# A decoder layer in one program: the order of stick-breaking steps, memory attention and dilated attention on TensorE

## The chip, the core and the metric

The kernel runs on one core of a Trainium2 chip. The metric is the device time of one execution in microseconds (us), median of several. A core has five engines with queues of their own: TensorE (PE in the profile, its weight loads PEld), VectorE (DVE), ScalarE (ACT), GpSimd (POOL) and SyncE (SP, which issues most transfers here). The engines wait for each other through semaphores, and each works through its own list strictly in the order in which it is written. TensorE multiplies a stationary tile of weights with a moving tile of columns into PSUM, which has four pairs of banks here (`ps[:, 0]` to `ps[:, 3]`, 1024 fp32 columns each).

## The reference

One layer over x (1024 positions, 1024 features), all in fp32:

```
x = x + 0.5 * swiglu(rmsnorm(x), ffn1)
h = rmsnorm(x);  q_sb,k_sb,v_sb, q_d,k_d,v_d, q_x, gates = split(h @ w_in)
A (stick-breaking, 6 heads of 64):  z = q k^T / 8
   a = where(s < t, exp(log_sigmoid(z) + sum over s' > s of log_sigmoid(-z)), 0);  o = a v
B (dilated attention, 3 groups x 2 heads, QK-norm, relative bias), combined by softmax denominators
C (memory attention, 4 heads, 256 tokens, QK-norm):  softmax(q mk^T) mv
merged = sum over branches of sigmoid(gate) * (o @ w_branch);  x = x + merged @ w_out
x = x + 0.5 * swiglu(rmsnorm(x), ffn2)
```

## The kernel before

Activations lie transposed (features on partitions, positions along the columns). A projection product takes each fp32 operand as a high and a low part in the fp32r type and adds three products (high by high, low by high, high by low); for one 128-row tile `k` of the contraction and 1024 positions that is six matmuls of 512 columns. Weights come one unit (128 x 1024) at a time: SyncE fetches `raw`, ScalarE writes its high part (`split_hi`), VectorE the low part (`split_lo`, line 1011), two units ahead.

The mixer has three stretches that concern us, each written out by hand as one list per engine.

**Stick-breaking** (36 steps `s`, three pairs of heads with 12 steps each). A step treats one block of 128 keys of two heads against up to 512 queries. The position inside its pair (0 to 11) sets the width of a head's part: 128, 256, 384, then five times 512, then 128, 256, 384, 512. A step consists of
- scores (`sb_scores`, TensorE, six matmuls with 64 rows, into `ps[:, s % 2]`); they wait for `sb_kept`, ScalarE's copy of the scores two steps earlier,
- ScalarE's |z|, exp, copy and ln (`sb_explog`), with two masks on GpSimd in the blocks on the diagonal; VectorE's softplus, high and low part (`sb_softplus`, lines 1277, 1284, 1286),
- `sb_within`: four matmuls with a triangle of ones that add to the running sum in `ps[:, 2]`; VectorE's add of that sum to the scores (`sb_add`, line 1293); ScalarE's exp of it, the weights (`sb_weights`, line 845),
- `sb_carry`: four more matmuls that complete the running sum; they wait for the add. VectorE may write the high part of step s+2 only behind them (line 1283),
- `sb_values`: weights by values, in fp32, two heads side by side of 64 columns each; they wait for the weights.

Beside the steps runs a projection of nine units: `beside(s, i, j)` multiplies tiles i to j of half a unit, three matmuls of 512 columns a tile, four tiles a step. Its result lies in one bank, which VectorE copies out at the end of each second step (`beside_copy`, line 1314). In that same bank values are turned (`v_turn`, copied out by `v_out`) and sums of squares of the memory queries are formed (`xq_sum`, copied out by `xq_keep`, followed by `xq_scale`).

**Memory attention** (8 pieces `n`) beside eight projections of 1024 positions: `x_turn` (eight fp32 transposes of the weights), `x_scores(n + 1)`, `x_values(n)`. Weights of piece n+1 are ready when VectorE has divided them (`x_divide`).

**Dilated attention** (32 blocks `n`) beside `fill(n)`, one contraction tile of a gate product: `d_scores` for two blocks at a time, `d_turn`, `d_values` for two blocks.

Of the kernel before, what the change touches and what calls it, by code (L numbers as in the profile page):

```python
# [25 lines left out]
P = 128  # L26
D = 1024
S = 1024
# [179 lines left out]
def is_v(half):  # L208
    return half is not None and half // 2 % 3 == 2
# [16 lines left out]
def layer(nc, x, mem, weights, gains, head_gains, rel_bias, consts, onehot, out):  # L226
    ctx = ExitStack()
    with ctx:
        base = -(-nc.sbuf_base // 64) * 64

        def at(name, off, shape, dt=F32):
            return nc.alloc_sbuf_tensor_at(name, shape, dt, offset=base + off)
# [79 lines left out]
        sp_hi = at("sp_hi", XT + 8 * K, [P, 2, 2, 512], F32R)  # L312
        sp_lo = at("sp_lo", XT + 16 * K, [P, 2, 2, 512], F32R)

        sb_a = [at(f"sb_a{i}", o, [P, 2, 512]) for i, o in enumerate((XT + 24 * K, XT + 28 * K, AR + 48 * K, AR + 28 * K))]

        tri = at("tri", MISC + 512, [P, 2, P], F32R)

# [93 lines left out]
        def after(eng, s, value):  # L412

            if not isinstance(value, int) or value > 0:
                eng.wait_ge(s, value)
# [35 lines left out]
            return ps[:, s % 2, :].rearrange("p (h c) -> p h c", h=2)  # L451

        def sb_weights_of(s):
            return sb_a[3 if s % 3 == 2 and s >= 2 * PAIR_STEPS else s % 3]

        def carry(h):

# [21 lines left out]
        def bank(i):  # L479
            return ps[:, i // 2, (i % 2) * 512:(i % 2) * 512 + 512]  # L480
# [153 lines left out]
        def _(act):  # L634
# [59 lines left out]
            def proj_square(n):  # L694

                kind, w = PROJ[n]
                pr_sq, pr_rs, pr_vT = pr_mem if n < PR_SB else pr_x
                if kind == "norm" and n >= PR_DIL:
                    act.wait_ge(pr_copied, n + 1)
                    after(act, pr_kept, kept_before(n))  # L700
                    nc.scalar.activation(sq_full[:], proj_dest(n), ACT.Square).then_inc(pr_sq_done, 1)
                    nc.scalar.activation(sq_hi[:], proj_dest(n), ACT.Square).then_inc(pr_sq_hi_done, 1)
                elif kind == "norm":
                    act.wait_ge(pr_copied, n + 1)

                    after(act, pr_final, aux_before(n))
                    nc.scalar.activation(pr_sq[:, 0:w], proj_dest(n), ACT.Square).then_inc(pr_sq_done, 1)
                elif kind == "copy":
                    act.wait_ge(pr_copied, n + 1)
                    nc.scalar.activation(sb_qk[:, 0, 2 * (n - PR_SB), :], proj_dest(n), ACT.Copy).then_inc(qk_hi_done, 1)  # L710
# [115 lines left out]
            def sb_explog(s):  # L826

                l, z = sb_l[:, s % 2, :, sb_step(s)[3]:], sb_scores_of(s)[:, :, sb_step(s)[3]:]
                act.wait_ge(sb_z, s + 1)
                after(act, sb_lo, s - 1)  # L830
                nc.scalar.activation(l, z, ACT.Abs).then_inc(sb_abs, 1)  # L831
                act.wait_ge(sb_abs, s + 1)
                nc.scalar.activation(l, l, ACT.Exp, scale=-1.0).then_inc(sb_exp, 1)  # L833
                after(act, sb_av, s - 2)
                nc.scalar.activation(sb_weights_of(s)[:, :, sb_step(s)[3]:], z, ACT.Copy).then_inc(sb_kept, 1)
                act.wait_ge(sb_exp, s + 1)
                if on_edge(s):
                    act.wait_ge(sb_exp_masked, edges_before(s) + 1)
                nc.scalar.activation(l, l, ACT.Ln, bias=1.0).then_inc(sb_ln, 1)
# [65 lines left out]
            for n in range(9):  # L905
                p = PR_DIL + n
                if n == 1:
                    act.wait_ge(xq_final, 4)
                if n:
                    proj_square(p - 1)  # L910
                if n < 8:
                    split_hi(proj_unit(p) + AHEAD)
                if n < 8:
                    for b in range(MB):
                        act.wait_ge(xa_turned, 2 * n + b + 1)
                        after(act, xa_pv, n)
                        nc.scalar.activation(x_pT[:, b, :], ps[:, 1, 512 * b:512 * b + 512], ACT.Copy).then_inc(xa_pT, 1)
                if n + 1 < 8:
                    x_exp(n + 1)
                if n:  # L920
                    proj_keep(p - 1)
                if n:
                    proj_rstd(p - 1)
# [81 lines left out]
        def _(dve):  # L1005
# [255 lines left out]
            def x_divide(n):  # L1261
                dve.wait_ge(xa_exp, 4 * n + 4)
                nc.vector.reciprocal(x_rden[:], x_den[:]).then_inc(xa_rden, 1)
                dve.wait_ge(xa_rden, n + 1)
                nc.vector.tensor_tensor(x_p[:], x_p[:], x_rden[:].unsqueeze(2).to_broadcast([P, 4, MEM]),
                                        ALU.mult).then_inc(xa_prob, 1)
# [117 lines left out]
            for n in range(9):  # L1384
                p = PR_DIL + n
                behind = n > 1 and PROJ[p - 2][0] == "norm"
                if behind and PROJ[p - 1][0] == "turn":
                    proj_final(p - 2)
                if n:
                    proj_copy(p - 1)  # L1390
                if behind and PROJ[p - 1][0] == "norm":
                    proj_final(p - 2)
                if n < 8:
                    split_lo(proj_unit(p) + AHEAD)
                if n == 0:
                    xq_scale(2)
                    xq_scale(3)
                if n + 1 < 8:
                    x_lowest(n + 1)
                    x_divide(n + 1)  # L1400
                if n < 8:
                    pair, quarter = divmod(n, 4)
                    dve.wait_ge(xa_pv, n + 1)
                    nc.vector.tensor_copy(o_x[:, pair, 256 * quarter:256 * quarter + 256], bank(2)[:, 0:256]).then_inc(xa_o, 1)
                if 0 < n < 8 and PROJ[p - 1][0] == "turn":
                    proj_final(p - 1)

# [138 lines left out]
        def _(pe):  # L1546
# [297 lines left out]
            def sb_scores(s):  # L1844

                p, c, j, a = sb_step(s)
                after(pe, sb_kept, s - 1)
                if s % PAIR_STEPS == 0:
                    pe.wait_ge(qk_done, 2 + 4 * p)
                for i, (k, q) in enumerate(((2, 0), (2, 1), (3, 0))):  # L1850
                    for h in range(2):
                        r = h * HD
                        last = mm(ps[:, s % 2, 512 * h + a:512 * h + 512], sb_qk[r:r + HD, p % 2, k, j * P:(j + 1) * P],
                                  sb_qk[r:r + HD, p % 2, q, 512 * c + a:512 * c + 512], i == 0, i == 2)
                last.then_inc(sb_z, 1)
# [75 lines left out]
                mm(xq_bank(q), head_r[:], xq_sq_lo[:, half_of(q)[1]], False, True).then_inc(xq_sums, 1)  # L1931

            proj(PR_SB, hh, hl)
            norm_sum(1)
            proj(PR_SB + 1, hh, hl)
            proj(PR_SB + 2, hh, hl)

            def x_scores(n):
# [12 lines left out]
            sb_scores(0)  # L1951
            sb_scores(1)
            proj_aux(PR_SB + 2)
            beside(0, 0, 4)
            for s in range(SB_STEPS):
                if s + 2 < SB_STEPS:
                    sb_scores(s + 2)
                if is_v(half_done(s - 1)):
                    v_turn(half_done(s - 1))
                if xq_at(s) is not None:  # L1960
                    xq_sum(xq_at(s))
                early = 0 if not s or is_v(half_done(s - 1)) or xq_at(s) is not None else 2
                if early:
                    beside(s, 0, early)
                if s:
                    sb_carry(s - 1)
                    sb_values(s - 1)
                if s:
                    beside(s, early, 4)
                else:  # L1970
                    pe.wait_ge(pr_final, aux_before(PR_DIL))
                sb_within(s)
# [43 lines left out]
            for n in range(8):  # L2016
                if n == 1:
                    pe.wait_ge(sb_o, 6)
                    pe.wait_ge(bs_v, 6)
                proj(PR_DIL + n, hh, hl, k1=DT // 2)  # L2020
                if n == 0:
                    sb_values(SB_STEPS - 1)
                x_turn(n)
                if n < 7:
                    x_scores(n + 1)
                proj(PR_DIL + n, hh, hl, k0=DT // 2, k1=DT - 2)
                if n:
                    proj_aux(PR_DIL + n - 1)
                x_values(n)
                proj(PR_DIL + n, hh, hl, k0=DT - 2)  # L2030

            pe.wait_ge(xa_exp, 32)
# [43 lines left out]
            for n in range(DN):  # L2076
                if n % 2 == 0 and n + 2 < DN:
                    d_scores(n + 2)
                if n % 8:
                    fill(n)  # L2080
                d_turn(n)
                if n == 2:
                    pe.wait_ge(pr_final, aux_before(len(PROJ)))
                if n % 2 == 0 and n:
                    d_values(n - 2)
                if n % 8 == 0 and n:
                    fill(n)
            d_values(DN - 2)

# [143 lines left out]
```

## Time and profile before

| what | us |
|---|---|
| median of 3 runs | 2343.32 (2341.65 to 2344.09) |
| the profiled execution's own time | 2342.55 |
| its span | 2340.8 |
| TensorE busy in the span | 2312.7 |
| stick-breaking loop, from 805.1 to 1027.3 | 222.2 |
| memory attention beside projections, from 1027.3 to 1150.0 | 122.7 |
| dilated attention, from 1150.0 to 1234.4 | 84.4 |

The granted clock of TensorE is 1.00 in all three stretches. A row of the timeline gives the start of a group of like instructions, how long the group takes and what the engine waited for; matmuls overlap, so what a group costs its engine is read from the start of the next row, not from its length.

### The profile page before, as it was taken

Reading aid. Unit: us, or ns where it says so; the run is one execution under the profiler, and the core shown is the slowest. Engines: PE = TensorE matmul, PEld = TensorE weight load, DVE = VectorE, ACT = ScalarE, POOL = GpSimd, SP = SyncE. Lnnn points to the kernel's source line nnn. Section 1 sums busy time; section 2 is a strip of 40 time slices with the busy share of each in tenths; the row PEclk is TensorE's granted clock in tenths of the full one; section 3 lists DMA queues with packets and bytes.
Section 4 is the critical chain, followed back from the end, with each engine's and each line's share of the span. In section 5 each row is a group of like instructions: output and inputs, shape, how many; then the busy total and the mean of one; then the engine's idle time right before and its main releaser. Section 6 shows DMA issues by size and latency. Waiting matters only on the chain.

```text
span 2340.8 us, 25824 instructions
## 1 busy us (share of the span) xinstructions
PE 2312.7 (99%) x10616; PEld 1859.5 (79%) x10616; DVE 1148.9 (49%) x1119; ACT 620.4 (27%) x800; POOL 137.6 (6%) x108
## 2 busy tenths in 40 slices
PE   8999999999999999999999999999999999999998
PEld 7888888888887766667778888888888888888887
DVE  8443444443445677777636343445344434444434
ACT  6211111111112567756443111223111111111111
POOL 3000000000001321212000000011000000000000
PEclk9999999999999999999999999999999999999999
DMA  5211111111112200001122111131111111111112
GB/s 161 76 45 54 45 49 40 54 45 54 45 54 61 108 28 19 19 28 55 37 28 64 54 54 45 55 117 53 47 52 48 45 54 45 48 42 54 45 54 72
DMA packets 47424, 125.78 MB, mean 54 GB/s; under 512 B 4285, under 2 KB 20829, under 8 KB 47104
## 3 DMA queue, kind: packets, MB, share of 16 engines
q1 hardware_dynamic: 45456, 112.61, 15.9%
q10 hardware_dynamic: 912, 10.11, 1.1%
q0 software_dynamic: 992, 2.15, 0.5%
q8 instruction: 48, 0.79, 0.1%
q14 instruction: 16, 0.13, 0.0%
HBM read 116.42 MB, written 9.87 MB: 54 GB/s over the span
## 4 chain that ended last, share of the span: by engine, by line
PE 93%; DVE 5%; ACT 1%; issue 1%; POOL 0%; DMA 0%; SPq 0%; DVEq 0%; ACTq 0%
PE ps L1548 91%; DVE h_lo L1018 1%; DVE w_lo L1011 0%; DVE sb_a L1293 0%; PE ps L2041 0%; DVE xT L1082 0%; DVE xT L1194 0%; DVE h_lo L1474 0%; PE ps L1984 0%; PE ps L2135 0%; DMA raw<-in_weights 0%; ACT sb_a L845 0%; ACT sb_l L833 0%; ACT sb_l L831 0%; PE ps L1757 0%
## 5 line engine op out<-in xcount | busy, mean ns | idle before, releaser
L1548 PE MATMUL ps<-h_hi,w_hi 128*128 128x512 f32 x2240 | 876.7, 396 | 2.7 <-ACT w_hi L641 2.3
L1548 PE MATMUL ps<-h_lo,w_hi 128*128 128x512 f32 x2240 | 862.6, 390 | 0.8 <-DVE h_lo L1474 0.4
L1548 PE MATMUL ps<-h_hi,w_lo 128*128 128x512 f32 x2240 | 699.9, 390 | 0.0
L1548 PEld LDWEIGHTS ps<-h_hi,w_hi 128*128 128x128 f32 x2240 | 420.2, 188 | 128.0 <-issue 40.5
L1548 PEld LDWEIGHTS ps<-h_hi,w_lo 128*128 128x128 f32 x2240 | 420.8, 188 | 88.9
L1548 PEld LDWEIGHTS ps<-h_lo,w_hi 128*128 128x128 f32 x2240 | 420.3, 188 | 85.8 <-DVE h_lo L1474 1.7
L641 ACT ACTIVATE w_hi<-raw 128x1024 fp32r<-128x1024 f32 x196 | 204.2, 1051 | 791.5 <-PE ps L1548 771.0
L1011 DVE TENSOR_TENSOR w_lo<-raw,w_hi 128x1024 fp32r<-128x1024 f32 x196 | 249.7, 1282 | 159.1 <-ACT w_hi L641 150.2
L1082 DVE TENSOR_TENSOR xT<-xT,ps 128x1024 f32<-128x1024 f32 x175 | 213.3, 1219 | 181.2 <-PE ps L1548 181.2
L1548 PE MATMUL ps<-a_hi,w_hi 128*128 128x512 f32 x704 | 276.8, 393 | 5.6 <-DVE w_lo L1011 4.9
L1548 PE MATMUL ps<-a_lo,w_hi 128*128 128x512 f32 x704 | 275.1, 391 | 0.0
L1548 PE MATMUL ps<-a_hi,w_lo 128*128 128x512 f32 x704 | 218.1, 391 | 0.0
L1048 DVE SCALAR_TENSOR_TENSOR glu<-ps,rB 128x1024 f32<-128x1024 f32 x44 | 53.9, 1224 | 265.1 <-PE ps L1548 265.1
L1041 DVE TENSOR_TENSOR silu<-ps,rB 128x1024 f32<-128x1024 f32 x44 | 53.8, 1224 | 252.1 <-PE ps L1548 252.1
L677 ACT ACTIVATE silu<-silu 128x1024 f32<-128x1024 f32 x44 | 46.6, 1060 | 439.6 <-DVE silu L1041 439.6
L1548 PEld LDWEIGHTS ps<-a_hi,w_hi 128*128 128x128 f32 x704 | 133.1, 189 | 35.3 <-DVE w_lo L1011 5.7
L1548 PEld LDWEIGHTS ps<-a_hi,w_lo 128*128 128x128 f32 x704 | 132.7, 189 | 27.8
L1548 PEld LDWEIGHTS ps<-a_lo,w_hi 128*128 128x128 f32 x704 | 133.0, 189 | 27.1
L567 POOL TENSOR_TENSOR acc<-acc,sq 128x1024 f32<-128x1024 f32 x21 | 51.9, 2470 | 1090.5 <-ACT sq L648 1090.5
L1414 DVE TENSOR_TENSOR gate<-ps,rB 128x1024 f32<-128x1024 f32 x24 | 29.4, 1224 | 128.2 <-PE ps L1548 128.2
L941 ACT ACTIVATE gate<-gate 128x1024 f32<-128x1024 f32 x24 | 25.0, 1058 | 172.7 <-DVE gate L1414 172.5
L1066 DVE TENSOR_TENSOR glu<-glu,silu 128x1024 f32<-128x1024 f32 x44 | 53.9, 1224 | 4.4
(224 smaller groups left out, 1589.4 us busy)
## 6 DMA issues: line engine op xcount, KB each, us to landing
raw<-in_weights SPq DMA_DIRECT2D x196, 512.0 KB, 3.5
x_keep<-xT ACTq DMA_DIRECT2D x1, 4096.0 KB, 12.3
x_back<-x_keep ACTq DMA_DIRECT2D x1, 4096.0 KB, 13.4
x_nat<-in_x SPq DMA_DIRECT2D x7, 512.0 KB, 7.4
out<-y_nat SPq DMA_DIRECT2D x7, 512.0 KB, 3.2
toe_keep<-toe_row ACTq DMA_DIRECT2D x2, 704.0 KB, 6.1
m_nat<-in_mem SPq DMA_DIRECT2D x1, 1024.0 KB, 8.4
d_fB<-d_f_keep POOLq DMA_DIRECT2D x2, 512.0 KB, 6.5
```

What stands on the lines that cost most here:

```text
L567: nc.gpsimd.tensor_tensor(acc[:], acc[:], sq[:, k % 2, :], ALU.add).then_inc(acc_done, 1)
L641: nc.scalar.activation(w_hi[:, k % NW].rearrange("p a b -> p (a b)"), raw[:, k % NRAW, :], ACT.Copy).then_inc(hi_done, 1)
L677: nc.scalar.activation(silu[:, t % 2, :], silu[:, t % 2, :], ACT.Silu).then_inc(silu_done, 1)
L941: nc.scalar.activation(gate_tile(m, b), gate_tile(m, b), ACT.Sigmoid).then_inc(gate_done, 1)
L1011: nc.vector.tensor_tensor(w_lo[:, k % NW].rearrange("p a b -> p (a b)"), raw[:, k % NRAW, :], w_hi[:, k % NW].rearrange("p a b -> p (a b)" ...
L1018: nc.vector.scalar_tensor_tensor(out=h_lo[:, k, :], in0=xT[:, k, :], scalar=g32[:, gain, k:k + 1], in1=h_hi[:, k, :].bitcast(F32), op0=ALU ...
L1041: nc.vector.tensor_tensor(silu[:, t % 2, :], ps[:, 0, :], rB[:], ALU.mult).then_inc(gate_scaled, 1)
L1048: nc.vector.scalar_tensor_tensor(out=glu[:, t % 2, :], in0=ps[:, 1, :], scalar=0.5, in1=rB[:], op0=ALU.mult, op1=ALU.mult).then_inc(up_sca ...
L1066: nc.vector.tensor_tensor(glu[:, t % 2, :], glu[:, t % 2, :], silu[:, t % 2, :], ALU.mult).then_inc(glu_done, 1)
L1082: nc.vector.tensor_tensor(xT[:, m, :], xT[:, m, :], ps[:, 2 + m % 2, :], ALU.add).then_inc(down_added, 1)
L1414: nc.vector.tensor_tensor(gate_tile(m, b), ps[:, merge_pair(m, b), :], rB[:], ALU.mult).then_inc(mg_taken, 1)
L1548: return pe.matmul(o, a, b, start=start, stop=stop, skip_group_check=True)
```

## The change

In the stick-breaking loop the scores of two steps and the values of two steps now stand together at the beginning of each even step. The tiles of the projection move accordingly (three between carry and within in even steps, three ahead of the carry and two behind it in odd ones). Six buffers for weights in place of four, and one of its own for the last step. The first tile of projection `PR_SB + 1` goes ahead of the norm's sum. In memory attention the turn stands behind the first tile of a projection (from the second one on), and the values directly behind the next scores; ScalarE's copies of the turned weights and VectorE's copy of the result move ahead. In dilated attention the values of two blocks stand directly behind the scores of two blocks, and each `fill` stands behind a turn. The values of the last two steps are in the middle of the first projection of the next stretch.

```diff
+        sb_a = [at(f"sb_a{i}", o, [P, 2, 512])
+                for i, o in enumerate((XT + 24 * K, XT + 28 * K, AR + 48 * K, AR + 52 * K, AR + 28 * K, AR + 32 * K))]
+        sb_a_end = at("sb_a_end", AR + 14 * K, [P, 2, S])[:, :, 0:512]
         def sb_weights_of(s):
-            return sb_a[3 if s % 3 == 2 and s >= 2 * PAIR_STEPS else s % 3]
+            if s == SB_STEPS - 1:
+                return sb_a_end
+            return sb_a[s % 4 + (2 if s % 4 > 1 and s >= 2 * PAIR_STEPS else 0)]
...
-                after(act, sb_av, s - 2)
+                after(act, sb_av, s - 3)
...
             proj(PR_SB, hh, hl)
+            proj(PR_SB + 1, hh, hl, k1=1)
             norm_sum(1)
-            proj(PR_SB + 1, hh, hl)
+            proj(PR_SB + 1, hh, hl, k0=1)
...
-            beside(0, 0, 4)
+            beside(0, 0, 3)
             for s in range(SB_STEPS):
-                if s + 2 < SB_STEPS:
+                odd = s % 2
+                if not odd and s + 2 < SB_STEPS:
                     sb_scores(s + 2)
+                    sb_scores(s + 3)
+                if not odd and s:
+                    sb_values(s - 2)
+                    sb_values(s - 1)
                 if is_v(half_done(s - 1)):
                     v_turn(half_done(s - 1))
                 if xq_at(s) is not None:
                     xq_sum(xq_at(s))
-                early = 0 if not s or is_v(half_done(s - 1)) or xq_at(s) is not None else 2
-                if early:
-                    beside(s, 0, early)
+                if odd:
+                    beside(s, -1, 2)
                 if s:
                     sb_carry(s - 1)
-                    sb_values(s - 1)
                 if s:
-                    beside(s, early, 4)
+                    beside(s, 2 if odd else 0, 4 if odd else 3)
                 else:
                     pe.wait_ge(pr_final, aux_before(PR_DIL))
                 sb_within(s)
...
-                proj(PR_DIL + n, hh, hl, k1=DT // 2)
+                proj(PR_DIL + n, hh, hl, k1=1)
+                if n:
+                    x_turn(n)
+                proj(PR_DIL + n, hh, hl, k0=1, k1=DT // 2)
                 if n == 0:
+                    sb_values(SB_STEPS - 2)
                     sb_values(SB_STEPS - 1)
-                x_turn(n)
+                if n == 0:
+                    x_turn(n)
                 if n < 7:
                     x_scores(n + 1)
+                if n:
+                    x_values(n)
...
-                x_values(n)
+                if n == 0:
+                    x_values(n)
...
-                if n % 8:
-                    fill(n)
-                d_turn(n)
                 if n == 2:
                     pe.wait_ge(pr_final, aux_before(len(PROJ)))
                 if n % 2 == 0 and n:
                     d_values(n - 2)
-                if n % 8 == 0 and n:
+                d_turn(n)
+                if n:
                     fill(n)
```

TensorE's list before, from the carry of step 14 to the beginning of step 16 (`sb_qk` are scores, `sb_a` by `sb_v` values, `sp` by `tri` carry or within, `h` by `w` tiles of the projection):

```order
L1548 MATMUL ps<-sp_lo,tri 128x384 x2
L1548 MATMUL ps<-sb_a_106,sb_v_100 64x384 x2
L1548 MATMUL ps<-h_hi,w_hi 128x512
...
L1548 MATMUL ps<-h_hi,w_lo 128x512
L1548 MATMUL ps<-sp_hi,tri 128x512 x2
L1548 MATMUL ps<-sp_lo,tri 128x512 x2
L1548 MATMUL ps<-sb_qk 128x512 x6
L1548 MATMUL ps<-h_hi,w_hi 128x512
```

Values and scores each stand alone there, with tiles or a carry around them. The same place now, from the carry of step 14 to that of step 15:

```order
L1556 MATMUL ps<-sp_lo,tri 128x384 x2
L1556 MATMUL ps<-h_hi,w_hi 128x512
...
L1556 MATMUL ps<-h_hi,w_lo 128x512
L1556 MATMUL ps<-sp_hi,tri 128x512 x2
L1556 MATMUL ps<-sp_lo,tri 128x512 x2
L1556 MATMUL ps<-sb_qk 128x512 x12
L1556 MATMUL ps<-sb_a_106,sb_v_100 64x384 x2
L1556 MATMUL ps<-sb_a_107,sb_v_100 64x512 x2
L1556 MATMUL ps<-sp_hi,tri 128x512 x2
```

The scores of two steps (x12) and the values of two steps stand behind each other between a within and a carry; before, each stood alone between other kinds.

TensorE's list in dilated attention before, between two turns of three blocks each (`cst` by `d_p` are turns, `d_qk` scores, `d_pT` by `d_v` values):

```order
L2041 MATMUL ps<-cst,d_p 128x128 x3
L1548 MATMUL ps<-d_qk 128x128 x2
L1548 MATMUL ps<-d_qk 128x256 x2
L1548 MATMUL ps<-h_hi,w_hi 128x512
...
L1548 MATMUL ps<-h_hi,w_lo 128x512 x2
L2041 MATMUL ps<-cst,d_p 128x128 x3
L1548 MATMUL ps<-d_pT,d_v 64x128 x6
```

Each turn has scores or values behind it, and these a fill. The same stretch now:

```order
L1556 MATMUL ps<-d_qk 128x256 x2
L1556 MATMUL ps<-d_pT,d_v 64x128 x6
L2061 MATMUL ps<-cst,d_p 128x128 x3
L1556 MATMUL ps<-h_hi,w_hi 128x512
...
L1556 MATMUL ps<-h_hi,w_lo 128x512 x2
L2061 MATMUL ps<-cst,d_p 128x128 x3
L1556 MATMUL ps<-h_hi,w_hi 128x512
```

Scores, values and a turn follow each other, and the other turn stands alone between two fills.

## Rows read from the trace of the kernel before

**Rows 1.** The page, busy us, share of the span, instructions.

```profile
PE 2312.7 (99%) x10616; PEld 1859.5 (79%) x10616; DVE 1148.9 (49%) x1119; ACT 620.4 (27%) x800; POOL 137.6 (6%) x108
```

**Rows 2.** Windows, the stick-breaking loop: busy us and count by engine, clock.

```profile
805.10:1027.30 222.20, 216.35 (x1057) 145.09 (x1056) 167.91 (x198) 160.81 (x209) 48.30 (x49) 1.00 0.07 22
```

**Rows 3.** Waits of PE, 770 to 1250: us in total, times, longest.

```profile
PE ps L1548 <- ACT sb_a L845: 4.0, 6, 1.1
PE ps L1548 <- POOL acc_lo L570: 1.6, 1, 1.6
PE ps L1548 <- DVE sb_a L1293: 1.2, 2, 1.0
PE ps L1548 <- ACT d_pT L823: 0.6, 1, 0.6
```

**Rows 4.** Timeline of PE: start us, length us, group, count [idle before].

```profile
905.98 0.97 PE L1548 MATMUL ps<-sb_qk 64*128 64x512 f32 x6
906.88 0.50 PE L1548 MATMUL ps<-h_hi,w_hi 128*128 128x512 f32 x1
907.22 0.40 PE L1548 MATMUL ps<-h_lo,w_hi 128*128 128x512 f32 x1
...
908.37 0.61 PE L1548 MATMUL ps<-sp_hi,tri 128*128 128x512 f32 x2
908.82 0.61 PE L1548 MATMUL ps<-sp_lo,tri 128*128 128x512 f32 x2
909.37 1.08 PE L1548 MATMUL ps<-sb_a,sb_v 128*64 128x512 f32 x4
910.38 0.50 PE L1548 MATMUL ps<-h_hi,w_hi 128*128 128x512 f32 x1
```

**Rows 5.** Timeline of PE: two scores together, and each kind alone.

```profile
799.94 0.96 PE L1548 MATMUL ps<-sb_qk 64*128 64x128 f32 x12
...
912.88 0.55 PE L1548 MATMUL ps<-sb_qk 64*128 64x128 f32 x6
...
919.36 0.62 PE L1548 MATMUL ps<-sb_qk 64*128 64x256 f32 x6
```

**Rows 6.** Timeline behind a within of 512 columns.

```profile
874.66 0.79 PE L1548 MATMUL ps<-sb_qk 64*128 64x384 f32 x6
874.77 1.22 DVE L1293 TENSOR_TENSOR sb_a<-sb_a,ps 128x1024 f32<-128x1024 f32 x1 [0.21 <-PE ps L1548]
...
877.13 1.08 PE L1548 MATMUL ps<-sb_a,sb_v 128*64 128x512 f32 x4 [1.10 <-ACT sb_a L845]
```

**Rows 7.** Timeline: from a carry's end (the values' start) through VectorE's list.

```profile
895.80 0.87 PE L1548 MATMUL ps<-sb_a,sb_v 128*64 128x384 f32 x4
...
899.58 1.21 DVE L1293 TENSOR_TENSOR sb_a<-sb_a,ps 128x1024 f32<-128x1024 f32 x1
...
902.48 1.08 PE L1548 MATMUL ps<-sb_a,sb_v 128*64 128x512 f32 x4
...
903.38 1.23 DVE L1286 TENSOR_TENSOR sp_lo<-sb_l,sp_hi 128x1024 fp32r<-128x1024 f32 x1
```

**Rows 8.** Timeline of DVE, steps 30 and 31: sums kept, next add.

```profile
989.60 0.69 DVE L1336 COPY xq_kept_sums<-ps 128x512 f32<-128x512 f32 x1
...
997.75 1.21 DVE L1293 TENSOR_TENSOR sb_a<-sb_a,ps 128x1024 f32<-128x1024 f32 x1
```

**Rows 9.** Lines, 805 to 1027: busy us, mean ns of one, idle before.

```profile
L1286 DVE TENSOR_TENSOR sp_lo<-sb_l,sp_hi 128x1024 fp32r<-128x1024 f32 x18 | 24.7, 1371 | 0.6
```

**Rows 10.** Timeline of DVE, from the last result to the second piece's weights.

```profile
1035.57 0.69 DVE L1300 COPY o_sb<-ps 128x512 f32<-128x512 f32 x1 [2.35 <-PE ps L1548]
...
1045.64 1.23 DVE L1265 TENSOR_TENSOR x_p<-x_p,small 128x1024 f32<-128x1024 f32 x1
```

**Rows 11.** Timeline of PE in dilated attention, a turn ahead of scores.

```profile
1195.22 0.49 PE L2041 MATMUL ps<-cst,d_p 128*128 128x128 f32 x3
1195.64 0.93 PE L1548 MATMUL ps<-d_qk 64*128 64x128 f32 x8
```

More of the change, by code:

```diff
@@ L313, in layer @@
         sp_lo = at("sp_lo", XT + 16 * K, [P, 2, 2, 512], F32R)
-        sb_a = [at(f"sb_a{i}", o, [P, 2, 512]) for i, o in enumerate((XT + 24 * K, XT + 28 * K, AR + 48 * K, AR + 28 * K))]
+        sb_a = [at(f"sb_a{i}", o, [P, 2, 512])
+                for i, o in enumerate((XT + 24 * K, XT + 28 * K, AR + 48 * K, AR + 52 * K, AR + 28 * K, AR + 32 * K))]
+        sb_a_end = at("sb_a_end", AR + 14 * K, [P, 2, S])[:, :, 0:512]
         tri = at("tri", MISC + 512, [P, 2, P], F32R)
@@ L908, in _ @@
                     act.wait_ge(xq_final, 4)
-                if n:
-                    proj_square(p - 1)
-                if n < 8:
+                if n == 0:
                     split_hi(proj_unit(p) + AHEAD)
@@ L917, in _ @@
                         nc.scalar.activation(x_pT[:, b, :], ps[:, 1, 512 * b:512 * b + 512], ACT.Copy).then_inc(xa_pT, 1)
+                if n:
+                    proj_square(p - 1)
+                if 0 < n < 8:
+                    split_hi(proj_unit(p) + AHEAD)
                 if n + 1 < 8:
@@ L1399, in _ @@
                     x_lowest(n + 1)
-                    x_divide(n + 1)
                 if n < 8:
@@ L1404, in _ @@
                     nc.vector.tensor_copy(o_x[:, pair, 256 * quarter:256 * quarter + 256], bank(2)[:, 0:256]).then_inc(xa_o, 1)
+                if n + 1 < 8:
+                    x_divide(n + 1)
                 if 0 < n < 8 and PROJ[p - 1][0] == "turn":
@@ L2028, in _ @@
                     proj_aux(PR_DIL + n - 1)
-                x_values(n)
+                if n == 0:
+                    x_values(n)
                 proj(PR_DIL + n, hh, hl, k0=DT - 2)
@@ L2085, in _ @@
                     d_values(n - 2)
-                if n % 8 == 0 and n:
+                d_turn(n)
+                if n:
                     fill(n)
```

## The prediction, made before the changed kernel ran

> **What bounds the kernel now.** I read the page first: TensorE is busy for 2312.7 of 2340.8 us [rows 1], so anything that doesn't shorten TensorE's list, or a wait in it, is worth nothing. Then the windows: in the stick-breaking loop TensorE is busy for 216.4 of 222.2 us, but VectorE has 167.9 and ScalarE 160.8 [rows 2], so they have a quarter of slack and no more. The list of waits says that TensorE waits little there, 4.0 us for weights and 1.2 us for adds, besides one wait of 1.6 us at the norm's sum and one of 0.6 us at the end of dilated attention [rows 3]. The busy share hides a cost, though, which only the starts in the timeline show. Inside one kind of full-width matmul the starts are 0.23 us apart (two in 0.45, from 908.37 to 908.82). The two before values take 0.55, so 0.10 more; six scores, which run as three pairs of heads, take 0.90 in place of 0.69; and the first projection matmul behind them takes 0.34 in place of 0.23 [rows 4]. So scores that stand alone cost 0.10 + 0.20 + 0.11 = 0.4 us beyond their columns. For values I take as bare time 0.213 us for each 128 columns, the step between 0.87 and 1.08 us, the lengths at 384 and 512 columns [rows 7]; 512 columns are 0.85, the row takes 1.01 [rows 4], and with the ends the overhead is 0.10 + 0.16 + 0.11, some 0.36 us.
>
> **Stick-breaking, what is saved.** Before, two steps hold two scores and two values apart: 2 x 0.40 + 2 x 0.36 = 1.52 us of overhead. Now there is one island. Two scores in a row exist in one place: twelve matmuls of 128 and 256 columns have a length of 0.96, the two alone 0.55 and 0.62, of which 0.07 is tail, so 1.10 together [rows 5]. That join saves 0.14 us beyond the ends, which I extend to wide ones at up to 0.2. Scores directly ahead of values don't exist in the trace: between 0 and 0.2 us; I take 0.15, since going from either kind to the full width costs about 0.2 [rows 4]. An island then costs 0.10 + 0.10 + 0.05 + 0.15 + 0.05 + 0.11, about 0.57, and two steps save 0.95. There are 16 such islands (steps 2 to 32), 15.2 us, and the ends of the loop (step 0, step 34, values of step 34 in the next stretch) give 0.35 each: **16.3 us saved**.
>
> The page TensorEngine Tiling (Array Packing) of the Trainium skill, section Key Properties, says that a change of the tiling mode drains TensorE while a change of tile within a mode does not. By that rule the joins of like kinds are free and the step from scores to values (other rows and columns) is not, as I take it; without a drain there the loop would gain 16 x 0.15 = 2.4 us more. No row here decides it.
>
> **Stick-breaking, what is lost.** The values of an odd step s-1 now stand a short way behind its own within. What must happen meanwhile is add, weights exp, and that takes 877.13 - 874.77 = 2.36 us from the add's start [rows 6]. Take step 4 of a pair and count from the end of within(3). TensorE reaches values(3) after 0.19 for the entry, six score pairs at 0.23 (1.39), 0.15, values(2) at 384 columns (0.64): 2.4 us. But the add doesn't start at once. In the odd step VectorE can begin the next high part only behind the carry, and the carry now stands behind three tiles (9 x 0.23 = 2.07) plus its own 0.70. From the end of a carry of 384 columns to the next add, through high part, low part, a unit's low part (line 1011, every second odd step) and the copy of the projection, it was 899.58 - 895.80 = 3.78 us [rows 7], hidden before because values and tiles stood behind the carry in a step of 6.7 us (902.48 - 895.80). Now the odd step ends at 2.07 + 0.70 + 1.38 + 0.91 = 5.06, and VectorE is free at 2.77 + 3.78 = 6.55, so the add starts at 1.49, the weights are there at 3.85, and **TensorE waits 1.45 us**. Behind that wait stand the carry, three tiles and the next within, so nothing hides it. Step 6 has no unit's low part: carry's end 2.98, high and low part 2.13 (904.61 - 902.48), copy 0.6, odd step 5.27, add at 0.46, weights at 2.8, against TensorE at 1.85 (its scores are 128 and 256 columns wide): 1.0 us. The same count, with chains shortened for narrow tiles by 0.7 us (estimate from lengths in proportion to columns), gives 0.9 at step 8, 0.7 at step 10, 1.1 at step 0 of a pair, none at step 2. At steps 10 and 0 the turned values block the projection's bank until VectorE has copied them (0.69 us for such a copy [rows 8], 0.8 with the way there); values and tiles stood between, now a short carry or none: 0.35 and 0.8 us. Sum for 12 steps 6.3, for the first twelve, which have no step 0 of the kind, 4.4.
>
> The last twelve have the memory queries too. VectorE needs 997.75 - 989.60 = 8.15 us from keeping the sums to the next add [rows 8], and the sums now come 3.3 us later in the step, since two scores and two values stand ahead. At step 30 that makes the add of step 30 end 12 to 14 us into the step, with the carry wanting it at 10.4; at step 32 it is about 1.3 us and 0.6 for the bank, and at step 34 there are no scores to cover the values: 1.7. With 1.45 and 1.9 for steps 28 and 24 I take 11.3 (9 to 14). All waits: 4.4 + 6.3 + 11.3 = 22.0 us, before 5.5 (4.0 + 1.2 of [rows 3] and 0.3 at a turn): **16.5 us lost**. So the loop as a whole stays where it was, 0.2 us slower. If VectorE were free at every within, the waits would be about 8 us; that is the other bound.
>
> **Norm's sum.** One tile (six matmuls, 1.38 us) goes into the wait of 1.6 us for the low part [rows 3], which ends by GpSimd's clock alone: **1.4 us saved**.
>
> **Memory attention.** Before, a piece has four changes of kind (turn to scores, scores to projection, to values, back), now three; turns between tiles of full width are no change. That is 0.2 x 7 = 1.4 us. The price: the second turn comes three tiles earlier and waits for its weights. VectorE takes from 1035.57 to 1046.87 = 11.3 us from the last stick-breaking result to them [rows 10]; TensorE now needs about 2.0 for turn and scores (an estimate: eight transposes at 0.11 [rows 11], and scores like one group of values [rows 4]), 4 x 1.38 for tiles, 1.0 for values, 1.38 for the first tile and 0.3 for changes: 10.2. So it waits 1.1 us, once; later pieces have their weights 2 us ahead. Net **0.3 us saved** (-1 to 1.5).
>
> **Dilated attention.** Scores stood behind a turn (0.42 us for three transposes, which take 0.11 each, [rows 11]) and ahead of a fill, values likewise: four changes for two blocks; now fill to scores, scores to values, values to turn: three. At 0.2 to 0.25 us over 15 double blocks 3.4 us. The last values waited 0.6 us for a copy [rows 3] and now have a fill ahead of them. I see no new wait: exp of a block is done one turn earlier. **4.0 us saved** (1 to 5).
>
> **Sum.** -0.2 + 1.4 + 0.3 + 4.0 = 5.5 us. The profiled execution's own time, 2342.55, becomes 2337.1; it is 0.8 under the median of the runs, so I predict 2337.8 for the median.
>
> **Rivals.**
> 1. The waits in the loop stay small (5 to 14 us). For: VectorE and ScalarE have slack over the loop [rows 2]. Against: [rows 7] puts the add behind a list whose length is known, and it would have to be 1 us shorter. With the waits as before the sum is 22.0 us, 2321.3; with half of the added ones 2329.6.
> 2. Slower. One mechanism: VectorE's list in odd steps, while GpSimd masks. The low part takes 1.37 us on average where it takes 1.23 alone [rows 9, 7], and the chain of [rows 8] holds such stretched operations. If masks and VectorE's list meet in most odd steps, add and carry come 0.5 to 1 us later in each of 17, 9 to 17 us: at 14 us the time is 2351.8. It is slower than before by more than the bound once all waits exceed 32 us, 1.9 a double step where I have 1.2. The page SBUF — State Buffer of the Trainium skill has VectorE and GpSimd lock a shared port pair for a whole instruction; the low part's 1.37 us against 1.23 agrees that some are held up.
> 3. The joins save nothing: each kind pays its 0.4 even side by side. Then the loop loses 16.5 and saves only where the projection's entry goes, 2347 to 2350. Against it stands the one row of twelve [rows 5].
>
> **Chances.** A measurement of this kernel can't tell 0.2% (4.7 us) from no change. Forecast 0.72, its own range 2331 to 2344: 0.41 of it under 2338.6, 0.31 within the bound. Rival 1 0.13, all faster. Rival 2 0.11, of it 0.04 within the bound. Rival 3 0.04, half within the bound. So faster 0.54, same 0.37, slower 0.09. The range 2328 to 2345 leaves out the far half of rival 1 and rivals 2 and 3.
>
> **What would show it.** Right: in the timeline the scores of two steps as one row of twelve with values behind and one change of kind between; in the waits of TensorE over the loop about 20 us for the weights (line 845), the longest where VectorE's unit low part lies ahead of the add; the loop again near 222 us; dilated attention near 80.5; one wait near 1 us at the second memory turn; no wait at the norm's sum. Wrong: waits for weights under 10 us (rival 1), joins that still take 0.4 us (rival 3), waits for adds ahead of carries in all odd steps (rival 2).

## The result: 2345.1 us, 0.13% slower, where 0.23% faster was forecast

| | before | after |
|---|---|---|
| median of 22 runs, us | 2342.9 (2339.4 to 2345.4) | 2345.1 (2343.7 to 2348.7) |
| ratio to before, 95% interval | | 1.0013 (1.0007 to 1.0019) |
| profiled execution, its span, us | 2342.55, 2340.8 | 2343.77, 2341.7 |

The change is within the 0.2% that was called no change, but its sign isn't the forecast one, and it lies just above the range (2328 to 2345). The page of the changed kernel, the line that answers to [rows 1]:

```profile
PE 2294.7 (98%) x10616; PEld 1857.4 (79%) x10616; DVE 1146.1 (49%) x1119; ACT 619.4 (26%) x800; POOL 132.7 (6%) x108
```

TensorE is busy 18 us less with the same 10616 instructions, in a span that isn't shorter: what was saved came back as waiting. (The ends of matmuls are modelled, so the 18 us are no measure of the saving; the starts below are.) The waits of TensorE in the stick-breaking loop (columns as in [rows 3], which has 4.0 and 1.2 us for the same two tiles):

```profile
PE ps L1556 <- ACT sb_a L850: 15.3, 16, 2.3
PE ps L1556 <- DVE sb_a L1300: 3.1, 2, 2.4
PE ps L1556 <- DVE sb_v L1336: 2.6, 4, 0.9
PE ps L1556 <- DVE xq_kept_sums L1343: 1.4, 2, 0.9
PE ps L1556 <- ACT sb_a L840: 1.2, 3, 0.7
```

And the window of the loop, which answers to [rows 2] (216.35 busy of 222.20):

```profile
801.31:1031.56 230.25, 206.51 (x1056) 148.16 (x1055) 165.72 (x199) 160.22 (x209) 44.15 (x50) 0.99 0.07 21
```

Cut into stages at the first matmul of each kind, with every start of TensorE taken singly from the trace (us; "half clock" is the time in the loop in which the granted clock stood at 0.5):

| | to the first scores | loop | memory | dilated | rest | half clock in the loop |
|---|---|---|---|---|---|---|
| before | 795.3 | 227.4 | 122.7 | 106.3 | 1080.5 | 0 |
| after | 792.6 | 234.7 | 123.1 | 104.1 | 1079.0 | 3.4 |
| e1, loop alone | 796.9 | 234.0 | 123.4 | 106.3 | 1079.0 | 3.4 |
| e2, the rest alone | 794.0 | 227.3 | 122.5 | 102.4 | 1080.5 | 0 |
| e3, list order | 792.3 | 232.7 | 124.1 | 102.5 | 1079.2 | 13.7 |
| e4, scores in pairs | 793.6 | 223.7 | 122.5 | 102.4 | 1080.5 | 0 |
| e5, unit's low part | 793.3 | 231.9 | 123.2 | 102.4 | 1080.6 | 10.2 |
| e6, values later | 794.2 | 222.4 | 123.8 | 102.3 | 1079.0 | 3.4 |
| e9, the best | 794.5 | 214.4 | 123.8 | 102.3 | 1080.6 | 3.4 |

The loop is 7.4 us longer. By steps: 1.3 us shorter over steps 0 to 3, 2.2 longer over 4 to 15, 1.0 longer over 16 to 27 (75.63 against 74.58 from the scores of step 14 to those of 26), 5.4 longer from 28 on, where the memory queries are. Three numbers of the table are in part not the change's: a fall of the clock explains up to 1.7 us of the loop, and falls that before had and after hasn't some 1.5 us each in the first and the last column (last section). The loop also holds fewer values in some kernels: those of step 34 stand behind it in the changed kernel, e1, e3 and e5, those of steps 32 to 34 in e6 and e9, which is why the column of memory attention is longer there. And dilated attention waited once, for 1.75 us, ahead of the scores at 1210.72, where VectorE and ScalarE stand still for 5.7 and 6.5 us; neither e2 nor any later kernel with the same code shows it (102.3 to 102.5 us in all of them), so it isn't the rule of this code, and why it came in this execution is open.

What a wait of the new kind looks like: timeline of the changed kernel at step 16 (start us, length us, [idle before]).

```profile
895.40 0.62 PE L1556 MATMUL ps<-sp_lo,tri 128*128 128x512 f32 x2
895.73 1.22 DVE L1018 TENSOR_TENSOR w_lo<-raw,w_hi 128x1024 fp32r<-128x1024 f32 x1
895.95 1.64 PE L1556 MATMUL ps<-sb_qk 64*128 64x512 f32 x12
896.86 0.69 DVE L1318 SCALAR_TENSOR_TENSOR pr_x<-ps,rB 128x512 f32<-128x512 f32 x1
897.46 1.21 DVE L1300 TENSOR_TENSOR sb_a<-sb_a,ps 128x1024 f32<-128x1024 f32 x1
897.52 0.87 PE L1556 MATMUL ps<-sb_a,sb_v 128*64 128x384 f32 x4
899.82 1.08 PE L1556 MATMUL ps<-sb_a,sb_v 128*64 128x512 f32 x4 [1.43 <-ACT sb_a L850]
```

The within of step 15 ends near 895.86 (second of two matmuls from 895.40). VectorE still has the unit's low part and the projection's copy ahead of its add, which starts at 897.46, 1.60 behind the within (forecast 1.49); the values follow 2.36 later, the very chain of [rows 6]. TensorE got to them at 897.52 + 0.64 = 898.16 (0.64 us is what values of 384 columns take, by the 0.213 us for each 128 columns of the prediction). So the wait is 1.66 us, and the view lists 1.43: it counts from the modelled end of the row before, which lies 0.2 us behind the moment at which the next matmul could have started. Below, a wait "by starts" is the distance from one matmul to the next, less what the columns of the first take by themselves; for this wait that gives 1.60, since values also lose 0.05 us between their own matmuls.

### The profile page after: what moved, and what is told of

Same layout as the page of the kernel before. It is cut to its first block, busy times and chain, and to the rows that moved or that the text cites. A ratio compares the mean times of both kernels' runs of the same rounds, so it can differ in the third digit from the quotient of the medians.

```text
span 2341.7 us, 25823 instructions
## 1 busy us (share of the span) xinstructions
PE 2294.7 (98%) x10616; PEld 1857.4 (79%) x10616; DVE 1146.1 (49%) x1119; ACT 619.4 (26%) x800; POOL 132.7 (6%) x108
## 4 chain that ended last, share of the span: by engine, by line
PE 53%; DVE 1%; issue 0%; another core or an unknown queue 0%; ACT 0%; DVEq 0%; ACTq 0%
PE ps L1556 52%; PE ps L2061 0%; DVE h_lo L1482 0%; PE ps L2153 0%; PE ps L1996 0%; DVE w_lo L1018 0%; DVE gate L1498 0%; DVE pr_x L1143 0%; PE ps L1765 0%; DVE d_p L1437 0%; ACT x_p L903 0%; DVE merged L1503 0%; DVE gate L1422 0%; DVE x_p L1272 0%
```

## Experiments

Ratios are to the kernel before, run beside each, with 95% intervals. "Middle pair" is the time from the scores of step 14 to those of step 26: 12 steps, in which no kernel had a fall of the clock.

### e1 and e2: the change in two

e1 is the kernel before with the edits of the stick-breaking loop alone, e2 with all the others (norm's sum, memory attention, dilated attention).

> The stick-breaking part of the change alone, on the kernel before. Theory A, read from the two traces: pairing saves about 14 us of starting overhead and the values of odd steps cost about 20 us of new waits, so this part alone is slower: the loop 5 to 6.5 us longer, the time 2348 to 2350 (ratio 1.002 to 1.003). Rival B, the loss comes from the parts acting on each other or from a clock dip in the one profile: the loop stays within 1 us of before and the time within 2341 to 2345, as the prediction's sum had it (+0.2).

> The other three parts alone (norm's sum, memory attention, dilated attention), with the stick-breaking loop of before. Theory A: they bring what the trace of the changed kernel shows for them, 1.3 + 0.4 + 2.2 = 3.9 us, so 2339 (ratio 0.9983); with the prediction's terms for them it would be 5.7 us, 2337.2. Rival B: they give under 1 us. If e1 and e2 add up to the whole change (+2.2 us), the parts don't act on each other.

Measured: e1 2349.4 us, ratio 1.0030 (1.0019 to 1.0042); e2 2335.1 us, ratio 0.9970 (0.9959 to 0.9981). Together +7.7 and -6.6, +1.1 us, and the whole change has +2.2 (interval 1.6 to 4.5): within their intervals, over 2 us each way, they add up. The stages say it closer: e1's loop is as long as the changed kernel's, 234.0 and 234.7, and e2's as long as that of before. e2's stages give norm's sum 1.4 us, memory 0.2, dilated 3.9: together 5.5, where the prediction had 1.4, 0.3 and 4.0. Rival B is out on both sides. Theory A for e2, 2339, was too high: it was read from the one trace of the changed kernel, in which dilated attention has the wait of 1.75 us. So nearly the whole miss is in the loop: +0.2 was forecast.

### e3 and e5: what stands ahead of the add

e5 moves one item of VectorE's list, the unit's low part, behind the add; e3 also moves the projection's copy.

```diff
@@ VectorE's loop over s (e3; e5 has only the split_lo lines)
                 if s:
                     sb_add(s - 1)
+                if half_done(s - 1) is not None:
+                    beside_copy(half_done(s - 1))
...
-                if s % 4 == 3:
-                    split_lo(beside_unit(s // 4) + AHEAD)
+                if s and s % 4 == 0:
+                    split_lo(beside_unit(s // 4 - 1) + AHEAD)
...
-                if half_done(s) is not None:
-                    beside_copy(half_done(s))
...
```

> The changed kernel with VectorE's list in another order alone: in odd steps the copy of the projection and the unit's low part go behind the add, not ahead of it. Theory A, the waits at the values come from what stands ahead of the add: the add starts 0.7 us sooner in every odd step and 1.2 us more in every second one, the waits at the values fall from about 15 us listed to 3 to 7, and the time falls by 9 to 14 us to 2331 to 2336. Rival C, the bare chain add then exp (2.4 us) is what TensorE can't cover: the waits stay over 11 us and the time within 3 us of 2345.

> The changed kernel with one item of VectorE's list moved: the unit's low part (1.2 us, every second odd step) goes behind the add. Theory A (the wait is what stands ahead of the add): the wait at step 4 of each pair falls from 1.4 us listed to 0.2 to 0.4, the waits at steps 6, 8, 10 and 0 stay as they are (0.8, 0.7, 0.6, 1.4), since they have no such item, and the loop is 3 to 4 us shorter. Rival C (the bare chain add, exp sets it): the waits at step 4 stay over 1 us.

Measured: e3 2340.7 us, ratio 0.9994 (0.9985 to 1.0003), against 1.0013 for the changed kernel; e5, one run, 2341.4. The waits in e5's loop and then in e3's:

```profile
PE ps L1557 <- DVE sb_a L1300: 6.4, 3, 3.0
PE ps L1557 <- ACT sb_a L850: 5.2, 12, 0.8
```

```profile
PE ps L1558 <- DVE sb_a L1300: 7.0, 5, 3.0
PE ps L1558 <- ACT sb_a L850: 3.5, 9, 0.8
```

The waits for weights fall from 15.3 to 5.2 us by the one item and to 3.5 by both; the middle pair falls from 75.63 to 72.90 and 72.98. So for the waits theory A holds, and over the middle pair the unit's low part alone is what mattered. My expectation for e5 had its places wrong, though: the item stands in steps 3, 7 and 11 of each pair, ahead of the values of steps 4, 8 and 0, and all three waits fell (by starts 1.60, 0.89 and 1.53 us in the changed kernel, 0.45, under 0.2 and 0.36 in e5). In e5 at step 16 the add starts at 894.46 with nothing but the projection's copy just ahead of it, and the wait is listed as 0.28.

```profile
893.86 0.68 DVE L1318 SCALAR_TENSOR_TENSOR pr_x<-ps,rB 128x512 f32<-128x512 f32 x1
894.46 1.21 DVE L1300 TENSOR_TENSOR sb_a<-sb_a,ps 128x1024 f32<-128x1024 f32 x1
...
896.81 1.08 PE L1557 MATMUL ps<-sb_a,sb_v 128*64 128x512 f32 x4 [0.28 <-ACT sb_a L850]
```

The rest of the gain came back in the last pair: waits for adds rose from 3.1 to 6.4 and 7.0 us, and with them the clock stood at half for 10.2 and 13.7 us, which costs up to 5 and 7 us, against 1.7. Together that is about the 5 to 10 us by which e3 misses its forecast of 2331 to 2336. Why the adds of the last pair wait longer there wasn't tested. e5 ran once, so its time has no interval.

### e4: pairs of scores, values single as before

```diff
...
-                if not odd and s:
-                    sb_values(s - 2)
-                    sb_values(s - 1)
...
-                if odd:
-                    beside(s, -1, 2)
+                early = 0 if not s or is_v(half_done(s - 1)) or xq_at(s) is not None else 2
+                if early:
+                    beside(s, 0, early)
                 if s:
                     sb_carry(s - 1)
+                    sb_values(s - 1)
...
```

> The changed kernel with the scores still in pairs, but the values single again behind the next carry, where they stood before, with two tiles ahead of each carry. Theory A: no wait for weights of the new kind, waits in the loop back near 7 us, and of the overhead only the join of two scores is saved, 0.4 us in each of 17 double steps, 7 us; with the other three parts (3.9) the time is 2332 to 2335. Rival C', the join of two scores brings nothing by itself (the saving sits in scores to values): 2338 to 2341.

Measured: 2334.2 us, ratio 0.9968 (0.9957 to 0.9979), and the listed waits are small again (4.2 for adds, 2.3 for weights). The time is as expected, but the join of two scores gives less: the loop is 3.6 us shorter, not 7, and the middle pair 2.25 (74.58 to 72.33), of which 0.5 is waits by starts (1.7 to 1.2 us), so 0.3 for each double step and not 0.4. Against e2 the runs gain only 0.9 us, with intervals of over 2 us each way, where the profiled loops differ by 3.6; that gap stays open. The values' side of the island is the larger saving, and e4 gives it up.

### e6, e7, e8: values still later

To keep the island and lose the wait, the values are held back until their weights are long there. It takes up to six buffers for weights of just the needed width (1 to 4 KB), put where a table says, each with the count of values that it waits for.

```diff
-                if not odd and s:
-                    sb_values(s - 2)
-                    sb_values(s - 1)
+                for t in sb_groups.get(s, ()):
+                    sb_values(t)
@@ sb_groups: {2: [0], 4: [1, 2], 6: [3, 4], 8: [5, 6], 10: [7], 12: [8, 9, 10], 14: [11], 16: [12, 13, 14], ...
@@ e7, even steps (ahead is 1 where neither a turn nor a sum of squares stands there):
+                elif ahead:
+                    beside(s, 0, ahead)
                 if s:
                     sb_carry(s - 1)
@@ e8: v_turn(...) ahead of the loop over sb_groups
```

> The changed kernel with the values one step later still: behind the scores of an even step s stand the values of s-3 and s-2 (groups that don't cross the end of a chain: 0; 1,2; 3,4; 5,6; 7; 8 to 10; 11), whose weights are ready. It takes up to six buffers for weights. Theory A: the waits for weights (19 us of starts too far apart) go, 1 to 5 us of them come back as waits for adds ahead of the carries that now stand directly behind the values; the saving of the pairs (about 15 us) stays. The loop is 216 to 222 us and the time 2327 to 2333. Rival D: the loss only changes its place, since VectorE's list in odd steps sets the pace: waits for adds over 12 us, the time over 2338.

> As the one before, with one of the three tiles of an even step ahead of its carry in place of behind it. Theory A: the waits for adds ahead of those carries go (0.7 us of cover each), 1 to 4 us less than the one before. Rival D: no change, or slower by what the later carry holds back on VectorE.

> As the one before, with the turn of the projected values ahead of the group of values in place of behind it (steps 12, 24 and 34), and a tile ahead of the carry there too. Theory A: the wait of 1.1 us for the copy behind the turn is covered by the values, minus 0.2 us for one more change of kind: 1 to 2 us less. Rival: the turn waits for the projection's copy, which is late itself: no gain or 1 us slower.

Measured: e6 2331.1 (ratio 0.9956, 0.9943 to 0.9970), e7 2331.3 (0.9956, 0.9942 to 0.9970), e8 2329.9 (0.9949, 0.9936 to 0.9963). No wait for weights is left in any; of e6's waits (the second line is scores that wait for a kept copy):

```profile
PE ps L1560 <- DVE sb_a L1303: 6.6, 6, 2.5
PE ps L1560 <- ACT sb_a L843: 2.6, 4, 1.3
```

For e6 that is theory A, though the waits for adds come to 6.6 us where I expected 1 to 5, and the loop is just over the edge (222.4, of which up to 1.7 by the clock, and without the values of steps 32 and 33). They also stand in other places than I expected: in the middle pair ahead of the carries of the odd steps 15 and 17 (0.72 and 1.05 us by starts), not of those directly behind the values. That is why e7's tile, which goes ahead of even carries, did nothing for the runs (middle pair 72.00 to 71.46): the two waits are still 0.71 and 1.03. So theory A for e7 missed, and the "no change" of rival D came out. e8 gains 1.4 us in the runs, within the noise of five runs, as expected. In its profile each of the first two pairs is 1.3 us shorter (the middle one 70.17), and the last is 2.6 longer: one more fall of the clock, and the turn of step 34 waits 1.26 us for the projection's copy, which is e8's rival in this one place.

### e9 and e10: the add again

In e8 VectorE itself waited in even steps, with the add behind the waiting instruction:

```profile
896.87 1.23 DVE L1296 TENSOR_TENSOR sp_lo<-sb_l,sp_hi 128x1024 fp32r<-128x1024 f32 x1
899.34 0.69 DVE L1330 TENSOR_TENSOR sb_qk<-pr_x,sb_qk 128x512 fp32r<-128x512 f32 x1 [1.24 <-ACT sb_qk L859]
899.95 1.22 DVE L1303 TENSOR_TENSOR sb_a<-sb_a,ps 128x1024 f32<-128x1024 f32 x1
```

```diff
@@ e9, VectorE's loop
                 if s:
                     sb_add(s - 1)
+                if is_qk(half_done(s - 2)):
+                    qk_lo(half_done(s - 2))
...
-                if is_qk(half_done(s - 1)):
-                    qk_lo(half_done(s - 1))
@@ e10, besides
-                if xq_at(s - 2) in (0, 1):
-                    xq_scale(xq_at(s - 2))
+                if xq_at(s - 3) == 0:
+                    xq_scale(0)
+                if xq_at(s - 2) == 1:
+                    xq_scale(1)
```

> The last kernel (values later, a tile ahead, turn ahead of the values) with the low part of the projected queries and keys moved from ahead of the add of the even step to behind it: VectorE waited 1.2 us there for ScalarE's high part. Theory A: the waits for adds at steps 3, 5 and 15, 17 of the loop (0.95, 1.2, 0.7, 1.0 us) go, since the add starts up to 1.9 us sooner: 3 to 4 us less, 2325.5 to 2328. Rival: the add is then held by the within ahead of it, and the waits only halve.

> As the one before, with the four scalings of the memory queries (2.5 us on VectorE) taken out of step 30, where the add of step 30 is behind them, into step 31 behind that add. Theory A: the wait of 2.3 us for that add falls under 0.5 and no other grows by more than 0.7, so 1.5 to 2.5 us less than the one before; if the half clock behind that wait (3.4 us of it) goes too, up to 1.7 us more. Rival: ScalarE's squares wait for the scalings, and hold back its weights: the wait moves to step 32, no gain.

Measured: e9 2325.9 us, ratio 0.9929 (0.9915 to 0.9943), the fastest of all and 16.6 us under the kernel before; e10 2326.7 (0.9931, 0.9918 to 0.9945). In e9 the middle pair has no wait at all and takes 67.59 us. The add stands ahead now:

```profile
896.18 1.22 DVE L1303 TENSOR_TENSOR sb_a<-sb_a,ps 128x1024 f32<-128x1024 f32 x1 [0.24 <-PE ps L1560]
897.47 0.69 DVE L1330 TENSOR_TENSOR sb_qk<-pr_x,sb_qk 128x512 fp32r<-128x512 f32 x1
```

e10's rival came true, and theory A missed. The wait for the add of step 30 is gone, but ScalarE's squares now wait for the scalings, with the kept copy of step 33 behind them, for which scores wait 3.6 us; the clock falls there for 6.8 us:

```profile
981.93 0.64 ACT L866 ACTIVATE pr_x<-x_q 128x512 f32<-128x512 f32 x1 [6.86 <-DVE x_q L1360]
```

```profile
987.65 1.65 PE L1562 MATMUL ps<-sb_qk 64*128 64x512 f32 x6 [3.60 <-ACT sb_a L843]
989.23 3.68 PE L1562 MATMUL ps<-sb_a,sb_v 128*64 128x512 f32 x8
```

## Why the prediction was wrong

**The step that failed is the one headed "Stick-breaking, what is lost"**: waits of 22.0 us in place of 5.5, 16.5 lost. The mechanism was the right one, the size was not. Counted by starts, as the prediction's chains were meant, the waits over 0.37 us in the loop come to 28.6 us in the changed kernel and 7.4 in the kernel before: some 21 us lost, not 16.5. Where the difference comes from:
- The waits at the values at steps 4, 6, 8 and 10 were near the forecast: 1.60, 0.94, 0.89 and 0.76 by starts, where I had 1.45, 1.0, 0.9 and 0.7. At step 0 it was 1.53 for 1.1, and at step 2, where I had none, 0.3 to 0.5. For step 0 I shortened the chain for narrow tiles and left out that the unit's low part, which is never narrow, stands in step 11 too. The 5.5 for the kernel before was taken from the list of waits [rows 3], which leaves some 0.2 us of each out, so it was too small.
- The turns at steps 12 and 24 cost 1.09 each where I had 0.8, those at 10 and 22 0.57 for 0.35.
- Scores that wait for a kept copy of ScalarE (0.91 us at step 2, 0.47 and 0.45 at steps 10 and 22) weren't in the sum at all: ScalarE must keep the scores of s + 1 before those of s + 3 are written.
- The last pair was put at 11.3 us and has 13.9. The terms named for it add up to only 8.6 to 10.6 (1.45, 1.9, 1.6 to 3.6, 1.3 + 0.6, 1.7), so 11.3 had a part with no term behind it; one wait without a term is that of 0.94 at the values of step 30. The wait for the add of step 30, listed as 2.35, is within the 1.6 to 3.6; the waits at steps 24, 28, 32 and 34 are some 0.3 to 1.5 us longer each.

**A term that wasn't there:** the half clock behind a wait, up to 1.7 us in this loop and up to 7 in e3. With 21.2 lost, 1.7 for the clock and 0.85 for the values of step 34, which moved out of the loop, the 7.4 us measured leave 14.7 us saved.

**Saved, 16.3 us: about right, 1.6 too much.** e9's middle pair has six islands too (with one to three values each) and no wait, 67.59 us from the first of these rows to the second:

```profile
867.30 0.79 PE L1560 MATMUL ps<-sb_qk 64*128 64x384 f32 x6
934.90 0.79 PE L1560 MATMUL ps<-sb_qk 64*128 64x384 f32 x6
```

Before it was 74.58 with about 1.7 us of waits. So six islands save 5.3 us, 0.9 each, where the prediction had 0.95; 0.3 of it is the pair of scores (e4), the rest the values and their join to the scores. Scores to values costs as much as any change of kind: the last score is 0.10 us farther from the values than its columns, the same 0.10 as from scores to tiles. So the gain of 2.4 us without such a cost is out. The page TensorEngine Tiling (Array Packing) of the Trainium skill says in Key Properties that a change of tiling mode drains TensorE; the 0.10 us agrees.

**The other parts** came as forecast, in e2's profile: 1.4, 0.2 and 3.9 us for 1.4, 0.3 and 4.0. The wait at the second memory turn is 1.00 (1.1 forecast); norm's sum kept 0.2:

```profile
1051.81 1.09 PE L1996 MATMUL ps<-cst,x_p 128*128 128x128 f32 x8 [1.00 <-DVE x_p L1272]
```

**The rivals.** Rival 1 (waits stay small) is refuted by the waits, rival 3 (the joins save nothing) by the islands. Rival 2 named the right direction, and said that the whole turns slower by more than the bound once all waits exceed 32 us: they were 28.6 by starts, and the time came out 2.2 us above before. Its mechanism, VectorE held up while GpSimd works, is in the trace as a part of the waits. At step 0 of the second pair:

```profile
869.59 0.89 DVE L1293 TENSOR_TENSOR sp_lo<-sb_l,sp_hi 128x256 fp32r<-128x256 f32 x1
870.41 1.76 DVE L1018 TENSOR_TENSOR w_lo<-raw,w_hi 128x1024 fp32r<-128x1024 f32 x1
869.47 0.74 POOL L585 TENSOR_TENSOR sb_l<-sb_l,cst 128x256 f32<-128x256 f32 x1 [6.09 <-ACT sb_l L838]
870.17 0.92 POOL L587 TENSOR_TENSOR sb_a<-sb_a,cst 128x256 f32<-128x256 f32 x1
```

Alone the first takes 0.42 us and the second 1.22. Of the nine low parts of units in the loop the five with a GpSimd instruction beside them take 1.75 or 1.76 us, the four without 1.22. By my estimate this is 0.5 us of the wait at step 8, 1.0 at step 0 and 1.0 of the one for the add of step 30, whose low part takes 2.21 us: some 4 to 5 us of the 21, and not the 9 to 17 on top that rival 2 had. The kernel before has such rows too, hidden. e5 takes the unit's low part out of the chain and with it both its length and its hold-up; no kernel separates the two. Against a sum of two terms of 16 us with opposite signs, a chance of 0.54 for faster was too high.

## What to carry to other kernels

When work is put together to save starts, ask for each consumer how long its producer's chain is from the last thing that both share, and look at the producer's own list first: here moving a single item of 0.7 to 1.2 us behind an add was worth some 3 to 4 us, twice (e5 by its one run, e9). Hold a consumer back by a step rather than let it wait, if buffers of the true width can be found: with that, e6 to e9 keep the saving that the change was after. And take waits from differences of starts, not from the listed idle, on an engine whose ends are modelled, and take off what the row before needs for its own columns.

## Not expected of the hardware

The granted clock of TensorE falls from 1.0 to 0.5 (2.4 to 1.2 GHz) for 3.4 us, in three cases for 6.8 or 10.2, and then matmuls of 512 columns start 0.43 us apart, not 0.23: up to 1.7 us are lost in each 3.4. In the twelve profiles there are 29 such falls behind the first 40 us and ahead of the last matmul, and every one began at a wait of TensorE of 1.7 us or more (by starts), between 1.3 us ahead of its end and 1.5 us behind it. In that stretch waits of 2.4 us and more had one in 26 of 37 cases, those of 1.6 to 2.3 us in 3 of 10. The same instruction with the same wait, before and then after:

```profile
738.77 0.79 PE L1548 MATMUL ps<-a_hi,w_hi 128*128 128x512 f32 x1 [2.45 <-DVE w_lo L1011]
739.36 0.63 PE L1548 MATMUL ps<-a_lo,w_hi 128*128 128x512 f32 x1
739.78 0.63 PE L1548 MATMUL ps<-a_hi,w_hi 128*128 128x512 f32 x1
```

```profile
738.59 0.50 PE L1556 MATMUL ps<-a_hi,w_hi 128*128 128x512 f32 x1 [2.45 <-DVE w_lo L1018]
738.92 0.39 PE L1556 MATMUL ps<-a_lo,w_hi 128*128 128x512 f32 x1
739.16 0.40 PE L1556 MATMUL ps<-a_hi,w_hi 128*128 128x512 f32 x1
```

In the changed kernel's loop it was the wait for the add of step 30:

```profile
999.53 1.03 PE L1556 MATMUL ps<-sp_hi,tri 128*128 128x512 f32 x2 [2.35 <-DVE sb_a L1300]
1000.36 1.06 PE L1556 MATMUL ps<-sp_lo,tri 128*128 128x512 f32 x2
```

and the longest, in e3, as a window (the seventh number behind the span is the clock):

```profile
1010.40:1020.60 10.20, 8.47 (x30) 6.32 (x31) 5.38 (x9) 5.93 (x7) 1.63 (x2) 0.50 0.17 52
```

Why one wait is followed by a fall and the same wait in another execution is not stays open; no kernel was made to tell it. What it means for a sum: a single wait of 2.4 us or more can cost up to 1.7 us once more, as it did here in most cases. Two profiles of one stretch differ by 1.5 to 1.7 us for this reason alone, which is the size of several terms of the prediction. So look up the clock of both before you compare a stage; the middle pair has it full in all kernels.
